# The first loads of a two-layer decoder trunk in another order: identity, one memory tile and one weight slot ahead of the rest

## The chip, the cores and the metric

The kernel runs on one core of one Trainium2 chip. The metric is the device time of one execution in microseconds (us); the time of a kernel is the median of several executions. A profiled execution gives besides its own time the span between its first and last instruction and a record of every instruction and DMA packet.

## The reference, cut to what matters

The program is a decoder trunk of two layers over 256 tokens with 1024 features. The parts that the start of the kernel computes are these:

```python
def memory_attention(q_mem, mem, w_mem_kv):
    kv = mem.astype(q_mem.dtype) @ w_mem_kv
    ...

def gla_group(h, mem, w_in, w_gk_up, b_gk, g_gla, w_mem_kv):
    q, k, v, g_out, gk_low, q_mem = jnp.split(h @ w_in, A_SPLITS, axis=-1)
    gk = jax.nn.log_sigmoid((gk_low @ w_gk_up + b_gk).astype(jnp.float32)) / GLA_GATE_NORM
    o = gla_chunked(q, k, v, gk)          # heads of 96 and 192 features, shapes left out
    o = rmsnorm(o, g_gla) * jax.nn.silu(g_out)
    m = memory_attention(q_mem, mem, w_mem_kv)
    ...

for l in range(2):
    h = rmsnorm(x, g_mix[l])
    mixed = gla_group(...) if l == 0 else diff_group(...)   # the second: differential attention
    x = x + mixed @ w_out[l]
    h = rmsnorm(x, g_ffn[l])
    x = x + (swiglu(h, ...) if l == 0 else moe_swiglu(h, ...))  # the second: top 2 of 8 experts
return rmsnorm(x, g_final)
```

`mem` has 256 rows of 1024 features, `w_mem_kv` is 1024 x 512 per layer, `w_gk_up` is 16 x 384 and `b_gk` has 384 elements.

## The kernel before

**Weights in slots.** Every weight matrix passes through SBUF in slots of 1 MB or less (128 partitions x up to 2048 elements). SP issues the loads into a ring of seven raw buffers (`raw`, semaphores `raw_in`); slot s may be loaded once the lower half of slot s - 7 has been made (`lo_ready`). ScalarE copies a raw slot to `w_hi` in the format fp32r (L395, which drops low bits), VectorE subtracts to get the rest, `w_lo` (L682). There are three such split buffers in the part before the experts, so ScalarE's split of slot s waits until TensorE has used slot s - 3 (`slot_used`). Each product is then three matmuls, hi x hi, lo x hi and hi x lo (`three`, L1130 to L1132).

**Activations.** Activations lie token-major in `H` (two tiles of 128 tokens). A `turn` transposes them on TensorE, eight 128x128 blocks a tile, against the identity `ident`, a block of the constants `cst`; ScalarE copies each half tile to `act_hi` (L406) and VectorE subtracts to `act_lo` (L695), in four quarters: two for each tile. A product that is feature-major waits for three quarters at its first step and for all four at its fifth (`await_turned`).

**The start.** Slots 0 to 3 are `w_mem_kv` of both layers, in halves of 256 columns, slot 4 holds the 16 gate-rank columns of `w_in_a`, slot 5 the memory queries, and slots 6 to 9 the queries and keys of the gated linear attention. The first turn is of `mem`, which SP loads into `H`. While TensorE computes keys and values of the memory from slots 0 to 3, ScalarE and VectorE compute the first layer norm: `norm` on ScalarE squares `xres` (the loaded x) with its sum and takes the root with `eps`, a column of `cst`; `norm` on VectorE waits for the gain (`gain_in`) and writes the result into `H`. On both engines this norm stands between the splits of slots 1 and 2, and each engine works through its program in order. The second turn is that of the normed x.

**Queues.** SP's queue carries all weights, `cst`, `mem` and x. GpSimd's queue carries the gain, broadcast to 128 partitions, and eight small tables that share the semaphore `small_in`: `wgk` (`w_gk_up`), `bgk` (the gate biases as 96 x 4), `ggla`, `gsub` and four lambda vectors, the last six broadcast to 128 partitions. TensorE waits for all eight before the four gate matmuls that follow slots 4 and 5:

```python
pe.wait_ge(small_in, N_SMALL)
for h in range(GH):
    ins = nc.tensor.matmul(ps[0:GDK, 6 + h // 2, S * (h % 2):S * (h % 2) + S],
                           wgk[:, GDK * h:GDK * h + GDK], gd[0:RANK, 0:S], start=True, stop=True)
```

After them ScalarE adds the bias in four operations (L479), and applies Abs, Exp and Ln; VectorE scans. The engines' order within each program is written out by hand.

The rest of the kernel (attention, dense part, shared keys and values, differential attention, router, and eight experts with 42 slots each) is not touched by the diff.

Of the kernel before, what the change touches and what calls it, by code (L numbers as in the profile page):

```python
# [24 lines left out]
P = 128  # L25
D = 1024
S = 256
# [69 lines left out]
def trunk(nc, x, mem, g_mix, g_ffn, w_mem_kv, w_out, w_in_a, w_gk_up, b_gk, g_gla, g_kv, w_kv, w_in_b,  # L97
# [7 lines left out]
    with ExitStack() as ctx:  # L105
# [17 lines left out]
        rsc = sb("rsc", [P, 5, TT, NE])  # L123
        bgk = sb("bgk", [GDK, GH])
        idx8 = sb("idx8", [P, TT, 8], U32)
# [60 lines left out]
        lam4 = sc[:, 0, 0:4 * HEAD_DIM].rearrange("p (i n) -> p i n", i=4)  # L186
        wgk = sc[0:RANK, 1, 0:GH * GDK]

# [14 lines left out]


        const_in = sem("const_in")
        small_in = sem("small_in")
        mem_in = sem("mem_in")
        x_in = sem("x_in")
# [12 lines left out]
        add_done = sem("add_done")  # L221
        gk_logit = sem("gk_logit")
        gk_act = sem("gk_act")
        gk_vec = sem("gk_vec")
# [83 lines left out]
        def _(sp):  # L308
            sp.dma_start(cst[:, :], consts).then_inc(const_in, 16)
            for t in range(TT):  # L310
                sp.dma_start(H[:, t, :], mem[0, P * t:P * t + P, :]).then_inc(mem_in, 16)
            for s, (src, k0, kt, n0, n) in enumerate(slots):
                if s == 2:
                    sp.dma_start(xres[:, :, :], x[0].rearrange("(t p) d -> p t d", p=P)).then_inc(x_in, 16)
                if s >= RAW:
                    sp.wait_ge(lo_ready, s - RAW + 1)
                with nc.allow_non_contiguous_dma(reason="router columns"):
                    sp.dma_start(shaped(raw, s % RAW, kt, n),
                                 src.rearrange("(k p) n -> p k n", p=P)[:, k0:k0 + kt, n0:n0 + n])\
                      .then_inc(raw_in[s % RAW], 16)  # L320
# [36 lines left out]
        def _(pool):  # L357
            gains = [g_mix[0:1, :], g_ffn[0:1, :], g_kv.rearrange("(a d) -> a d", a=1), g_mix[1:2, :],
                     g_ffn[1:2, :], g_final.rearrange("(a d) -> a d", a=1)]
            pool.dma_start(gain[:, :], gains[0].to_broadcast([P, D])).then_inc(gain_in, 16)  # L360
            pool.dma_start(wgk, w_gk_up[0]).then_inc(small_in, 16)
            with nc.allow_non_contiguous_dma(reason="384 gate biases"):
                pool.dma_start(bgk[:, :], b_gk[0].rearrange("(h p) -> p h", p=GDK)).then_inc(small_in, 16)
            pool.dma_start(ggla[:, :], g_gla[0:1, :].to_broadcast([P, GDV])).then_inc(small_in, 16)
# [12 lines left out]
        def _(act):  # L377
# [22 lines left out]

            def turn():
                n = turns[0]
                for t in range(TT):
                    for half in range(2):
# [3 lines left out]
                            ps[:, 2 * t + half, :].rearrange("p (k n) -> p k n", k=4), ACT.Copy).then_inc(turn_hi, 1)  # L408
                turns[0] += 1

# [40 lines left out]
            def attention(u0, u1, slots_end):  # L451
                for i in range(u0, u1 + 4):
# [6 lines left out]
                    if u0 <= i - 4:  # L459
                        unit_square(i - 4)  # L460

            split_to(1)
            turn()
            split_to(2)
            norm(x_in, (16, 16))
            for l in range(2):
# [5 lines left out]
            a = first["in_a"]  # L472

            proj(a + 1, gd[0:RANK, 0:S], ps[0:RANK, 4, 0:S])
            proj(a + 2, qmT[:, :, :], ps[:, 5, :].rearrange("p (m s) -> p m s", m=2))
            act.wait_ge(small_in, N_SMALL)
            act.wait_ge(gk_logit, 1)
            for h in range(GH):
                ins = nc.scalar.activation(ge[:, S * h:S * h + S], ps[0:GDK, 6 + h // 2, S * (h % 2):S * (h % 2) + S],  # L479
                                           ACT.Identity, bias=bgk[:, h:h + 1])  # L480
            ins.then_inc(gk_act, 1)
            act.wait_ge(gk_act, 1)
# [183 lines left out]
        def _(dve):  # L666
# [21 lines left out]

            def turn():
                n = turns[0]  # L690
                for t in range(TT):
                    for half in range(2):
# [4 lines left out]
                            act_hi[:, ks, P * t:P * t + P].bitcast(F32), ALU.subtract).then_inc(turn_lo, 1)  # L697
                turns[0] += 1

# [86 lines left out]
            def head_roots(n):  # L786

                link(nc.vector.reciprocal(hrs[:, n], hrms[:, n]))

            link(nc.vector.memset(ones[:, :], 1.0))  # L790
            link(nc.vector.memset(ki, 1.0))
            link(nc.vector.memset(ki[:, 0:D:CHUNK], 0.0))
            split_to(1)
            turn()
            split_to(2)
# [331 lines left out]
        def _(pe):  # L1127
# [18 lines left out]
            def turn():  # L1146

                for t in range(TT):
                    if turns[0] == 0:
                        pe.wait_ge(mem_in, 16 * TT)  # L1150
                    else:
                        pe.wait_ge(h_ready, TT * (turns[0] - 1) + t + 1)
# [46 lines left out]

            pe.wait_ge(const_in, 16)  # L1200
            turn()
# [16 lines left out]
            for h in range(GH):  # L1218
                ins = nc.tensor.matmul(ps[0:GDK, 6 + h // 2, S * (h % 2):S * (h % 2) + S],
                                       wgk[:, GDK * h:GDK * h + GDK], gd[0:RANK, 0:S], start=True, stop=True)  # L1220
            ins.then_inc(gk_logit, 1)
# [345 lines left out]
```

## Time and profile before

| | |
|---|---|
| median of 3 executions | 1589.26 us (1587.1 to 1592.56) |
| the profiled execution, its own time | 1586.55 us |
| its span | 1584.8 us |
| mean granted TensorE clock over the span | 0.952 |
| bytes moved by DMA | 428.34 MB, mean 270 GB/s |

Times in the trace count from the start of the span. An engine executes its instructions in order, so a row's start is the later of the end of its predecessor and of its waits. PEclk is the share of full TensorE clock that was granted; full is 2.4 GHz and 0.50 is 1.2 GHz. SPq and POOLq are issuing engines: the time beside a DMA issue is that of issuing it, not of the transfer.

### The profile page before, as it was taken

The page shows a single profiled execution, that of the slowest core. Times are in us where ns is not written, and L with a number is a line of the kernel's source. Part 1 is how long each engine was busy: PE and PEld are TensorE (multiplying, and loading weights), DVE is VectorE, ACT ScalarE, POOL GpSimd, SP SyncE. Part 2 cuts the span into 40 slices and gives each one's busy share as a digit, 9 for nine tenths or more (in the row PEclk, how much of TensorE's full clock was granted, in tenths as well). Part 3 has the DMA queues.
Part 4 walks back from the last instruction along what each step waited for, and adds up shares of the span by engine and source line. Part 5 has one row for each costly group of instructions (what it writes and reads, how often), then busy time and mean ns, then how long its engine had stood idle before and what let it go on. Part 6 is the DMA issues. An engine that isn't in the chain of part 4 may idle for free.

```text
span 1584.8 us, 19889 instructions
## 1 busy us (share of the span) xinstructions
PE 1499.1 (95%) x7534; PEld 1252.8 (79%) x7534; DVE 1144.9 (72%) x941; ACT 957.8 (60%) x868; POOL 7.9 (1%) x18
## 2 busy tenths in 40 slices
PE   4997899998978789999999999999999999999996
PEld 4995689998865668888887887887888888888885
DVE  3453454545557479879879878988887987987984
ACT  4553244334445377766767677767767677766773
POOL 1000000000000000000000000000000000000000
PEclk8995799999985899999999999999999999999998
DMA  9561154565512159989989999998997998998990
GB/s 295 184 206 53 54 169 164 187 209 185 165 54 80 53 195 384 387 298 375 387 319 347 385 334 335 384 376 287 394 376 288 384 380 289 385 385 285 380 384 29
DMA packets 201923, 428.34 MB, mean 270 GB/s; under 512 B 8848, under 2 KB 42672, under 8 KB 201872
## 3 DMA queue, kind: packets, MB, share of 16 engines
q1 hardware_dynamic: 200736, 424.18, 74.2%
q0 software_dynamic: 1136, 3.47, 0.9%
q8 instruction: 34, 0.56, 0.1%
q14 instruction: 17, 0.14, 0.0%
HBM read 426.57 MB, written 1.05 MB: 270 GB/s over the span
## 4 chain that ended last, share of the span: by engine, by line
PE 91%; DVE 5%; ACT 2%; DMA 1%; issue 1%; SPq 0%; DVEq 0%; ACTq 0%
PE ps L1130 27%; PE ps L1132 27%; PE ps L1131 27%; PE ps L1448 2%; PE ps L1426 2%; PE ps L1469 2%; DVE w_lo L682 1%; PE ps L1274 1%; DMA raw<-in_w_mem_kv_dram 1%; PE ps L1156 1%; PE ps L1249 1%; ACT w_hi L395 0%; PE ps L1327 0%; DVE small L739 0%; ACT sc L431 0%
## 5 line engine op out<-in xcount | busy, mean ns | idle before, releaser
L1063 DVE TENSOR_TENSOR e_wlo<-raw,e_whi 128x2048 fp32r<-128x2048 f32 x336 | 750.7, 2285 | 113.6 <-ACT e_whi L618 113.4
L618 ACT ACTIVATE e_whi<-raw 128x2048 fp32r<-128x2048 f32 x336 | 620.7, 1915 | 43.5 <-PE ps L1132 43.5
L1130 PE MATMUL ps<-e_whi,act_hi 128*128 128x512 f32 x1344 | 534.4, 398 | 2.9 <-DVE act_lo L1030 1.5
L1132 PE MATMUL ps<-e_wlo,act_hi 128*128 128x512 f32 x1344 | 523.9, 390 | 0.0
L1131 PE MATMUL ps<-e_whi,act_lo 128*128 128x512 f32 x1344 | 523.2, 389 | 0.0
L1130 PEld LDWEIGHTS ps<-e_whi,act_hi 128*128 128x128 f32 x1344 | 252.4, 188 | 57.5 <-issue 5.3
L1131 PEld LDWEIGHTS ps<-e_whi,act_lo 128*128 128x128 f32 x1344 | 252.6, 188 | 54.5 <-issue 3.8
L1132 PEld LDWEIGHTS ps<-e_wlo,act_hi 128*128 128x128 f32 x1344 | 252.3, 188 | 53.5
L682 DVE TENSOR_TENSOR w_lo<-raw,w_hi 128x2048 fp32r<-128x2048 f32 (+2 forms) x68 | 148.4, 2198 | 159.3 <-ACT w_hi L395 159.2
L395 ACT ACTIVATE w_hi<-raw 128x2048 fp32r<-128x2048 f32 (+2 forms) x68 | 124.1, 1839 | 105.7 <-PE ps L1132 89.7
L623 ACT ACTIVATE act_hi<-ps 128x512 fp32r<-128x512 f32 x56 | 33.5, 598 | 199.0 <-PE ps L1469 199.0
L1130 PE MATMUL ps<-act_hi,w_hi 128*128 128x256 f32 (+3 forms) x480 | 137.1, 286 | 14.5 <-DVE act_lo L695 14.5
L1131 PE MATMUL ps<-act_hi,w_lo 128*128 128x256 f32 (+3 forms) x480 | 136.8, 285 | 0.0
L1132 PE MATMUL ps<-act_lo,w_hi 128*128 128x256 f32 (+3 forms) x480 | 136.8, 285 | 0.0
L1130 PEld LDWEIGHTS ps<-act_hi,w_hi 128*128 128x128 f32 (+3 forms) x480 | 89.9, 187 | 16.7 <-issue 16.0
L1131 PEld LDWEIGHTS ps<-act_hi,w_lo 128*128 128x128 f32 (+3 forms) x480 | 90.0, 187 | 0.7
L1132 PEld LDWEIGHTS ps<-act_lo,w_hi 128*128 128x128 f32 (+3 forms) x480 | 89.9, 187 | 0.4
L1130 PE MATMUL ps<-w_hi,act_hi 128*128 128x512 f32 (+1 forms) x240 | 87.5, 365 | 0.2 <-DVE act_lo L695 0.2
L1131 PE MATMUL ps<-w_hi,act_lo 128*128 128x512 f32 (+1 forms) x240 | 87.1, 363 | 0.0
L1132 PE MATMUL ps<-w_lo,act_hi 128*128 128x512 f32 (+1 forms) x240 | 87.0, 362 | 0.0
L544 ACT ACTIVATE T<-ps 128x512 f32<-128x512 f32 x11 | 6.6, 597 | 85.8 <-PE ps L1132 85.8
L1068 DVE TENSOR_TENSOR act_lo<-ps,act_hi 128x512 fp32r<-128x512 f32 x56 | 38.5, 688 | 19.3 <-ACT act_hi L623 19.3
(200 smaller groups left out, 1116.9 us busy)
## 6 DMA issues: line engine op xcount, KB each, us to landing
raw<-in_w_exp_gate_dram SPq DMA_DIRECT2D x112, 1024.0 KB, 7.0
raw<-in_w_exp_up_dram SPq DMA_DIRECT2D x112, 1024.0 KB, 7.2
raw<-in_w_exp_down_dram SPq DMA_DIRECT2D x112, 1024.0 KB, 7.5
raw<-in_w_dense_gate_dram SPq DMA_DIRECT2D x11, 1024.0 KB, 5.2
raw<-in_w_dense_up_dram SPq DMA_DIRECT2D x11, 1024.0 KB, 5.4
raw<-in_w_dense_down_dram SPq DMA_DIRECT2D x11, 1024.0 KB, 5.7
raw<-in_w_out_dram SPq DMA_DIRECT2D x8, 1024.0 KB, 5.0
raw<-in_w_in_a_dram SPq DMA_DIRECT2D x7, 1024.0 KB, 6.6
```

Source lines behind the costliest of these rows:

```text
L395: nc.scalar.activation(w_hi[:, s % SPLIT, 0:kt * n], raw[:, s % RAW, 0:kt * n], ACT.Copy)\
L618: nc.scalar.activation(e_whi[:, (s - NPRE) % E_SPLIT, :], raw[:, s % RAW, :], ACT.Copy)\
L623: nc.scalar.activation(h_hi, ps[:, 4, :].rearrange("p (m n) -> p m n", m=4), ACT.Copy)\
L682: nc.vector.tensor_tensor(w_lo[:, s % SPLIT, 0:kt * n], raw[:, s % RAW, 0:kt * n], w_hi[:, s % SPLIT, 0:kt * n].bitcast(F32), ALU.subtract)\
L1063: nc.vector.tensor_tensor(e_wlo[:, r, :], raw[:, s % RAW, :], e_whi[:, r, :].bitcast(F32), ALU.subtract).then_inc(lo_ready, 1)
L1068: nc.vector.tensor_tensor(h_lo, ps[:, 4, :].rearrange("p (m n) -> p m n", m=4), h_hi.bitcast(F32), ALU.subtract).then_inc(e_lo, 1)
L1130: nc.tensor.matmul(dst, l_hi, r_hi, start=start, stop=False)
L1131: nc.tensor.matmul(dst, l_lo, r_hi, start=False, stop=False)
L1132: return nc.tensor.matmul(dst, l_hi, r_lo, start=False, stop=stop)
L1426: ins = nc.tensor.matmul(ps[:, 1 + 2 * half, P * k:P * k + P], H[:, t, c:c + P], oh[:, t, :], start=(t == 0), stop=(t == TT - 1))
L1448: nc.tensor.matmul(ps[:, SCATTER_BANKS[2 * t + n], :], ohT[:, P * t:P * t + P], y_e[:, 512 * n:512 * n + 512], start=True, stop=True).then ...
L1469: ins = nc.tensor.transpose(ps[:, 4, P * m:P * m + P], e_h[:, P * m:P * m + P], ident)
```

## The change

The constants are loaded in two pieces, the identity first and the remaining 705 columns after slot 1. SP's order becomes identity, memory tile 0, slot 0, memory tile 1, slot 1, other constants, x, slot 2. Each memory tile has a semaphore of its own, so tile 0 can be transposed alone; ScalarE and VectorE take the two quarters of tile 0 ahead of slot 0 and the two of tile 1 behind it. GpSimd issues the gain only when memory tile 1 is in, and the small tables only when x is in. The gate bias is loaded as row 16 under the 16 rows of `wgk`, and a row of ones, set by a memset on VectorE, lies under the gate activations `gd`; so the gate matmuls contract over 17 rows and add the bias, and ScalarE's four bias operations become one copy.

```diff
         lam4 = sc[:, 0, 0:4 * HEAD_DIM].rearrange("p (i n) -> p i n", i=4)
-        wgk = sc[0:RANK, 1, 0:GH * GDK]
+        wgk = sc[0:RANK + 1, 1, 0:GH * GDK]
 
...
 
+        ident_in = sem("ident_in")
         const_in = sem("const_in")
         small_in = sem("small_in")
-        mem_in = sem("mem_in")
+        mem_in = [sem(f"mem_in{t}") for t in range(TT)]
         x_in = sem("x_in")
...
         def _(sp):
-            sp.dma_start(cst[:, :], consts).then_inc(const_in, 16)
-            for t in range(TT):
-                sp.dma_start(H[:, t, :], mem[0, P * t:P * t + P, :]).then_inc(mem_in, 16)
+            with nc.allow_non_contiguous_dma(reason="the identity is a block of the constants"):
+                sp.dma_start(ident, consts[:, C_ID:C_ID + P]).then_inc(ident_in, 16)
+            sp.dma_start(H[:, 0, :], mem[0, 0:P, :]).then_inc(mem_in[0], 16)
             for s, (src, k0, kt, n0, n) in enumerate(slots):
+                if s == 1:
+                    sp.dma_start(H[:, 1, :], mem[0, P:2 * P, :]).then_inc(mem_in[1], 16)
                 if s == 2:
+                    with nc.allow_non_contiguous_dma(reason="the other blocks of the constants"):
+                        sp.dma_start(cst[:, C_IOTA:C_N], consts[:, C_IOTA:C_N]).then_inc(const_in, 16)
                     sp.dma_start(xres[:, :, :], x[0].rearrange("(t p) d -> p t d", p=P)).then_inc(x_in, 16)
...
                      g_ffn[1:2, :], g_final.rearrange("(a d) -> a d", a=1)]
+            pool.wait_ge(mem_in[1], 16)
             pool.dma_start(gain[:, :], gains[0].to_broadcast([P, D])).then_inc(gain_in, 16)
-            pool.dma_start(wgk, w_gk_up[0]).then_inc(small_in, 16)
-            with nc.allow_non_contiguous_dma(reason="384 gate biases"):
-                pool.dma_start(bgk[:, :], b_gk[0].rearrange("(h p) -> p h", p=GDK)).then_inc(small_in, 16)
+            pool.wait_ge(x_in, 16)
+            pool.dma_start(wgk[0:RANK, :], w_gk_up[0]).then_inc(small_in, 16)
+            pool.dma_start(wgk[RANK:RANK + 1, :], b_gk[0:1, :]).then_inc(small_in, 16)
             pool.dma_start(ggla[:, :], g_gla[0:1, :].to_broadcast([P, GDV])).then_inc(small_in, 16)
...
 
-            def turn():
+            def turn(tiles=range(TT)):
                 n = turns[0]
-                for t in range(TT):
+                for t in tiles:
                     for half in range(2):
...
                             ps[:, 2 * t + half, :].rearrange("p (k n) -> p k n", k=4), ACT.Copy).then_inc(turn_hi, 1)
-                turns[0] += 1
+                    turns[0] += t == TT - 1
 
...
 
+            turn(range(0, 1))
             split_to(1)
-            turn()
+            turn(range(1, TT))
             split_to(2)
+            act.wait_ge(const_in, 16)
             norm(x_in, (16, 16))
...
 
+            act.wait_ge(one_row, 1)
             proj(a + 1, gd[0:RANK, 0:S], ps[0:RANK, 4, 0:S])
             proj(a + 2, qmT[:, :, :], ps[:, 5, :].rearrange("p (m s) -> p m s", m=2))
-            act.wait_ge(small_in, N_SMALL)
             act.wait_ge(gk_logit, 1)
-            for h in range(GH):
-                ins = nc.scalar.activation(ge[:, S * h:S * h + S], ps[0:GDK, 6 + h // 2, S * (h % 2):S * (h % 2) + S],
-                                           ACT.Identity, bias=bgk[:, h:h + 1])
-            ins.then_inc(gk_act, 1)
+            nc.scalar.activation(ge.rearrange("p (b n) -> p b n", b=2), ps[0:GDK, 6:8, :], ACT.Copy).then_inc(gk_act, 1)
             act.wait_ge(gk_act, 1)
...
 
-            def turn():
+            def turn(tiles=range(TT)):
                 n = turns[0]
-                for t in range(TT):
+                for t in tiles:
                     for half in range(2):
...
                             act_hi[:, ks, P * t:P * t + P].bitcast(F32), ALU.subtract).then_inc(turn_lo, 1)
-                turns[0] += 1
+                    turns[0] += t == TT - 1
 
...
 
+            nc.vector.memset(gd[0:2 * RANK, 0:S], 1.0).then_inc(one_row, 1)
             link(nc.vector.memset(ones[:, :], 1.0))
...
             link(nc.vector.memset(ki[:, 0:D:CHUNK], 0.0))
+            turn(range(0, 1))
             split_to(1)
-            turn()
+            turn(range(1, TT))
             split_to(2)
...
                     if turns[0] == 0:
-                        pe.wait_ge(mem_in, 16 * TT)
+                        pe.wait_ge(mem_in[t], 16)
                     else:
...
 
-            pe.wait_ge(const_in, 16)
+            pe.wait_ge(ident_in, 16)
             turn()
...
                 ins = nc.tensor.matmul(ps[0:GDK, 6 + h // 2, S * (h % 2):S * (h % 2) + S],
-                                       wgk[:, GDK * h:GDK * h + GDK], gd[0:RANK, 0:S], start=True, stop=True)
+                                       wgk[:, GDK * h:GDK * h + GDK], gd[0:RANK + 1, 0:S], start=True, stop=True)
             ins.then_inc(gk_logit, 1)
```

SP's queue from the start of the program before the change (`H<-in_mem_dram` is the memory, `raw<-in_w_mem_kv_dram` slots 0 to 3, `xres` is x):

```order
L309 DMA cst<-in_consts_dram 128x833
L311 DMA H<-in_mem_dram 128x1024 x2
L318 DMA raw<-in_w_mem_kv_dram 128x8x256 x2
L314 DMA xres<-in_x_dram 128x2x1024
L318 DMA raw<-in_w_mem_kv_dram 128x8x256 x2
L318 DMA raw<-in_w_in_a_dram 128x8x16
```

and with the change:

```order
L311 DMA cst<-in_consts_dram 128x128
L312 DMA H<-in_mem_dram 128x1024
L323 DMA raw<-in_w_mem_kv_dram 128x8x256
L315 DMA H<-in_mem_dram 128x1024
L323 DMA raw<-in_w_mem_kv_dram 128x8x256
L318 DMA cst<-in_consts_dram 128x705
L319 DMA xres<-in_x_dram 128x2x1024
L323 DMA raw<-in_w_mem_kv_dram 128x8x256 x2
L323 DMA raw<-in_w_in_a_dram 128x8x16
```

The identity (128 columns) is alone in front, slot 0 stands between the memory tiles, and the other 705 columns of constants go with x behind slot 1.

ScalarE from the start of its program before the change:

```order
L395 ACT_TABLE_LOAD
L395 ACTIVATE w_hi<-raw 128x2048
L406 ACTIVATE act_hi<-ps 128x4x128 x4
L395 ACTIVATE w_hi<-raw 128x2048
L415 ACTIVATE H,small<-xres 128x1024
L416 ACT_TABLE_LOAD
L416 ACTIVATE small<-small,cst 128x1
L415 ACTIVATE H,small<-xres 128x1024
L416 ACTIVATE small<-small,cst 128x1
```

and with the change:

```order
L412 ACT_TABLE_LOAD
L412 ACTIVATE act_hi<-ps 128x4x128 x2
L401 ACTIVATE w_hi<-raw 128x2048
L412 ACTIVATE act_hi<-ps 128x4x128 x2
L401 ACTIVATE w_hi<-raw 128x2048
L421 ACTIVATE H,small<-xres 128x1024
L422 ACT_TABLE_LOAD
L422 ACTIVATE small<-small,cst 128x1
L421 ACTIVATE H,small<-xres 128x1024
L422 ACTIVATE small<-small,cst 128x1
```

Two of the four act_hi quarters moved ahead of the split of slot 0; the layer norm (rows on `xres` and `small`) stays behind the split of slot 1. VectorE's act_lo quarters move likewise.

## Rows read from the trace of the kernel before

**Rows 1.** The page: engine busy times, and the chain that ended last by engine.

```profile
PE 1499.1 (95%) x7534; PEld 1252.8 (79%) x7534; DVE 1144.9 (72%) x941; ACT 957.8 (60%) x868; POOL 7.9 (1%) x18
...
PE 91%; DVE 5%; ACT 2%; DMA 1%; issue 1%; SPq 0%; DVEq 0%; ACTq 0%
```

**Rows 2.** Chain that ended last, 0 to 30 us: start, duration, what.

```profile
2.14 15.84 DMA raw<-in_w_mem_kv_dram
...
18.00 1.92 ACT w_hi L395
...
20.02 2.29 DVE w_lo L682
22.31 1.81 DVE act_lo L695 x3
...
24.25 0.55 PE ps L1130
```

**Rows 3.** Timeline of TensorE, 9 to 13 us: start, duration, what, idle before.

```profile
9.30 3.65 PE L1156 MATMUL ps<-cst,H 128*128 128x128 f32 x16 [9.30 <-DMA H<-in_mem_dram]
```

**Rows 4.** Timeline of SP's queue, 0 to 200 us.

```profile
0.75 0.40 SPq L309 DMA_DIRECT2D cst<-in_consts_dram  x1
1.20 0.90 SPq L311 DMA_DIRECT2D H<-in_mem_dram  x2
2.14 2.42 SPq L318 DMA_DIRECT2D raw<-in_w_mem_kv_dram  x2
4.60 8.30 SPq L314 DMA_DIRECT2D xres<-in_x_dram  x1
```

**Rows 5.** DMA queues from 8.5 to 13.5 us: packets, MB, share of 16 engines.

```profile
DMA packets 441, 0.46 MB, mean 93 GB/s; under 512 B 61, under 2 KB 382, under 8 KB 441
...
q0 software_dynamic: 120, 0.13, 75.6%
q1 hardware_dynamic: 321, 0.33, 19.2%
```

**Rows 6.** DMA from 14 to 18 us.

```profile
DMA packets 1402, 1.45 MB, mean 363 GB/s; under 512 B 37, under 2 KB 1379, under 8 KB 1402
```

**Rows 7.** DMA issues, 0 to 14 us: KB each, us to landing (median).

```profile
xres<-in_x_dram SPq DMA_DIRECT2D x1, 1024.0 KB, 18.8
gain<-in_g_mix_dram POOLq DMA_DIRECT2D x1, 512.0 KB, 7.4
cst<-in_consts_dram SPq DMA_DIRECT2D x1, 416.5 KB, 3.1
...
sc<-in_lambda_k_dram POOLq DMA_DIRECT2D x2, 32.0 KB, 9.2
```

**Rows 8.** Timeline of ScalarE, 27.5 to 70 us.

```profile
33.06 1.91 ACT L395 ACTIVATE w_hi<-raw 128x2048 fp32r<-128x2048 f32 x1 [3.59 <-PE ps L1132]
...
44.57 1.92 ACT L395 ACTIVATE w_hi<-raw 128x2048 fp32r<-128x2048 f32 x1 [4.96 <-PE ps L1132]
...
64.05 1.55 ACT L479 ACTIVATE T<-ps,bgk 96x256 f32<-96x256 f32 x4
65.64 1.06 ACT L483 ACTIVATE T<-T 96x1024 f32<-96x1024 f32 x1
```

**Rows 9.** Windows: length, busy by engine; PEclk, DMA share, GB/s.

```profile
24.00:30.50 6.50, 6.25 (x29) 6.28 (x30) 6.43 (x8) 5.41 (x8) 0.51 (x1) 0.51 1.05 311
30.50:41.00 10.50, 10.50 (x90) 10.50 (x89) 3.98 (x3) 3.19 (x4) 0.03 (x1) 1.00 1.09 342
60.00:70.00 10.00, 10.00 (x78) 9.16 (x77) 2.25 (x3) 7.76 (x10) 0.00 (x0) 1.00 0.71 228
```

**Rows 10.** Timeline of VectorE, 27.5 to 32 us.

```profile
29.61 2.28 DVE L682 TENSOR_TENSOR w_lo<-raw,w_hi 128x2048 fp32r<-128x2048 f32 x1
```

**Rows 11.** Timeline of GpSimd's queue, 0 to 30 us.

```profile
1.91 0.51 POOL L361 DMA_DIRECT2D sc<-in_w_gk_up_dram  x1
...
5.78 0.54 POOL L367 DMA_DIRECT2D sc<-in_lambda_k_dram  x1
```

More of the change, by code:

```diff
@@ L123, in trunk @@
         rsc = sb("rsc", [P, 5, TT, NE])
-        bgk = sb("bgk", [GDK, GH])
         idx8 = sb("idx8", [P, TT, 8], U32)
@@ L222, in trunk @@
         gk_logit = sem("gk_logit")
+        one_row = sem("one_row")
         gk_act = sem("gk_act")
```

## The prediction

> **What bounds the kernel now.** I read the page first: TensorE is busy 95% of the span and holds 91% of the chain that ended last [rows 1]. So time can only go where TensorE waits. The longest such wait is the first one, and all moved instructions lie there, so I read the chain of waits from zero next: the first weight slot is issued at 2.14 us and lands at 18.00; ScalarE's upper half of it takes 1.92, VectorE's lower half 2.29, three of the four act_lo quarters 1.81, and the first product starts at 24.25 [rows 2]. The two memory tiles were there long before: the transposes start at 9.30, when the second tile lands [rows 3]. So the slot's landing releases everything, and the question is why 1 MB takes 15.8 us.
>
> The issues on SP's queue say what is ahead of it: the constants (416.5 KB), both tiles (1 MB), then slots 0 and 1, then x, whose issue is held until 12.9 [rows 4]. The queues say what happens beside it. Between 8.5 and 13.5 us q0, which carries GpSimd's tables, holds 75.6% of the sixteen engines' time for 120 packets and 0.13 MB; q1, with the weights, gets 19.2% and moves 0.33 MB [rows 5]. From 14 to 18, with q0 nearly empty, the mean is 363 GB/s [rows 6]. At that rate q1 would have moved 1.8 MB in those 5 us, so the table loads cost about 1.5 MB, or 4.1 us, just ahead of slot 0's landing. The four 32 KB lambda broadcasts are the last, landing 9.2 us after issue [rows 7].
>
> After 24.25 TensorE is continuously fed: ScalarE's splits at 33.06 and 44.57 start only when TensorE has used up a slot [rows 8], and the stretch 60 to 70 is full [rows 9]. A TensorE that starts earlier therefore keeps its lead, if slots keep coming.
>
> **The change part by part.** *Slot 0 lands earlier.* Ahead of its end stand 64 + 512 + 1024 KB, 1.64 MB, and no GpSimd transfer, since the gain waits for tile 1. The old constants, 0.43 MB, were in at 0.75 + 3.1 = 3.85 [rows 4, 7]. I let the new order have moved the same 0.43 MB by then; the other 1.21 MB at 363 GB/s take 3.3: 7.2 us, and I take 7.4 because the slowest engine ends a transfer. Upper bound: 1.48 MB were in only at 9.30 before, with q0 alongside [rows 3]; with the missing 0.16 MB that is 9.75. No row excludes 7.2 as the lower one.
>
> *The chain behind it.* ScalarE's two and VectorE's two quarters of tile 0 now lie before slot 0: tile 0 is in near 4.3, eight transposes are half of 3.65 [rows 3], done by 6.2, its copies by 6.9. After the landing: 1.92 + 0.10 + 2.29, then only one quarter instead of three, 0.60, and 0.13 of hand-over: 5.04 instead of 6.25. Tile 1 lands near 7.2 + 1.4 = 8.7, its first quarter is copied by 10.3, while VectorE is still in w_lo until 11.7. First product: 7.4 + 5.04 = 12.4. Against 24.25 that is 11.8 us earlier; with the bounds, 9.5 to 12.0.
>
> *Does the lead survive slot 2?* Before it stands the layer norm. x now follows 4.63 MB of its own queue and shares with 0.52 MB of gain: 3.85 + 4.72/0.363 = 16.9. The gain, issued near 8.8, took 7.4 before [rows 7], so 16.2: no later than x. Before, x landed at 4.60 + 18.8 = 23.4 and slot 2's lower half ended at 29.61 + 2.28 = 31.9, 8.5 later [rows 4, 7, 10]; so now 25.4. TensorE wants slot 2 where it wanted it before, 11.8 earlier: two slots took 44.57 - 33.06 = 11.5 [rows 8], so slot 2 began at about 38.6, now 26.8. Slack 1.4: no stall, but little more lead would be usable. The second constants transfer (352 KB) is within these bytes and the sqrt that reads its eps comes after x.
>
> *And slot 3?* It lands near 22.7 (two more MB at 363). Its limit: TensorE wants it at 44.3 - 11.8 = 32.5, less 4.4 for both halves: 28.1. The deferred tables start when x is in. Before, 6.6 us passed from the first table issue at 1.91 [rows 11] to the slow stretch; so it comes at 23.5 to 28.5. If slot 3 is caught by all of its 4.1 us it lands at 26.8, still 1.3 in time. Its cover is the 5.75 us that each slot feeds TensorE.
>
> *The rest.* The tables are first read by the gate matmuls, ahead of ScalarE's bias step at 64.05 [rows 8], now near 52. Their eight issues take 5.78 - 1.91 [rows 11], so the last comes near 21, and with 9.2 it lands at 30. Hidden by 20 us; until x is in, GpSimd holds nothing else back, its next gain being wanted only after the first layer norm's reader. The bias row replaces four ScalarE operations, 1.55 together, by one of 96x1024, like the Abs at 1.06 [rows 8]: 0.5 less on ScalarE, while TensorE is full with the next slots [rows 9]; without that cover it would be a gain of 0.5, so the bounds are 0 and 0.5 and I take 0. The matmuls' 17 rows instead of 16: no row shows it; the moving columns are the same, I take 0. The 32x256 memset stands ahead of VectorE's first wait, under the loads: 0. The extra issue on SP: 0.45 us, as between the first two [rows 4], already behind slot 0.
>
> *The clock.* 24.0 to 30.5 was granted 0.51, the lower level, 1.2 GHz: 29 matmuls in 6.25 us, 0.216 each; afterwards, at 1.00, 90 in 10.5, 0.117 each [rows 9]. How long the low level lasts behind the new start no row tells. Bounds: not at all, 29 x 0.099 = 2.9 less, and twice as long, 2.9 more; I take the same.
>
> Sum: 1586.55 - 11.8 = 1574.8 for the profiled execution. That one lies 2.7 below the median of the three runs, 1589.26, so the median becomes 1577.5.
>
> **A rule weighed.** What the trace shows is that SP's slot lands late while q0's packets occupy the engines [rows 5]. The Trainium skill, DMA: Bandwidth & Descriptors, section Queues, rings and completion order, says that each engine takes turns between queue rows packet by packet, and that a transfer's semaphore write lands after all earlier writes of that engine, across queues; by that rule the trace agrees, and it speaks against the change as much as for it, since deferred tables hold up slots 2 and 3 in the same way: that is rival A. The same page, Rules for kernel authors, advises coalescing small transfers, under 64 KB being mostly overhead, and the 64 KB identity is cut out of a larger one: rival B.
>
> **The rivals.** *A, the slow stretch stalls slot 3.* For: it must fall somewhere. Against: 1.3 us of slack after its full price. Were it twice as long (8.2), slot 3 would land at 30.9, 2.8 late: 1580.3.
> *B, the split costs in series.* SP's landings overlap (issues 0.45 apart), against it. Were the identity's fixed time paid ahead of tile 0, slot 0 would be later by at most 3.1 - 1.2 = 1.9, cst's time from issue to landing [rows 7] less 1.2 for its bytes: 1579.4. Bytes and slot 0 shift alike, so nothing gives this back.
> *C, the slow stretch belongs to slot 0's own first reads,* not to the tables. For: its packets begin in that stretch. Against: q0's 75.6%. Then slot 0 takes from tile 0's landing (4.3) the 8.7 it took from 9.30 to 18.00: 13.0, gain 5.0 + 1.2: 1583.1.
> *D, the clock is high from the first product:* 2.9 less, but slot 2 would then be wanted at 23.9 and comes at 25.4, which gives 1.5 back: 1576.1.
> *E, slower: the clock stays low.* TensorE now begins with two separate bursts of eight transposes and may be granted 1.2 GHz through slots 0 to 3. From 30.4 to 50 some 168 matmuls x 0.099 = 16.6 more: 1594.1. It decides from 119 matmuls on. Against: before, the level rose after 6.1 us of products from the same idle start.
>
> **How the numbers follow.** My forecast, 1577.5, has 73% (its own range 1574 to 1580.5); A 8%, B 5%, C 6%, D 5%, E 3%. The range takes in A to D, the bound of 9.75 for slot 0 (1579.8) and 2 us for the spread of a median (the three runs span 5.5): 1572 to 1583. Faster means over 0.3%, 4.8 us, about what a measurement of this kernel can tell from no change: below 1584.5. The main case and A to D lie there, except late ends of C: 92% faster, 5% the same, 3% slower.
>
> **What would show it.** Right: slot 0's split on ScalarE near 7.4, the first product near 12.4, slot 3's chain without a wait on a DMA, ScalarE's gate step near 52 and every later stage 11 to 12 earlier. A: a ScalarE wait on raw behind slot 2 and a TensorE gap near 32. C: 1 KB loads slow with q0 empty. E: PEclk near 0.5 beyond 20. Wrong as a whole: later stages that do not move with the first.

## The result and the profile after

The changed kernel takes 1597.8 us (median of 4 executions, 1596.49 to 1598.68) against 1588.18 (1585.01 to 1592.56): ratio 1.0058, 95% interval 1.0032 to 1.0084. It is 0.6% slower, where a gain to 1577.5 was forecast. The profiled execution took 1597.82 with a span of 1596.0, so its span is 11.2 longer than that of before.

The start went nearly as forecast. The chain that ended last, over the first microseconds, answers to [rows 2]:

```profile
1.66 6.89 DMA raw<-in_w_mem_kv_dram
8.58 1.92 ACT w_hi L401
10.52 2.29 DVE w_lo L687
12.82 0.61 DVE act_lo L700
...
13.56 0.55 PE ps L1137
14.11 0.21 PE ps L1138
...
17.32 0.21 PE ps L1138
17.53 0.19 PE ps L1139
...
21.34 0.12 PE ps L1138
```

Slot 0 lands at 8.55 instead of 17.98, 6.89 us behind its issue instead of 15.84; one act_lo quarter stands between its lower half and the first product instead of three, and that product starts at 13.56 instead of 24.25. The matmuls step by 0.21 us until 17.5 and by 0.12 afterwards; the granted column reads 1.00 from 13.5 on in this trace, so here the steps tell the level, not the column: before, 0.216 us a matmul stood beside a granted 0.51, and 0.117 beside 1.00 [rows 9]. The tables' slow stretch is now at 22 to 27, in the DMA queues of that window:

```profile
DMA packets 1631, 0.81 MB, mean 163 GB/s; under 512 B 1040, under 2 KB 1575, under 8 KB 1631
...
q0 software_dynamic: 191, 0.24, 60.8%
q1 hardware_dynamic: 1440, 0.57, 43.2%
```

q0 holds 60.8% of the engines' time for 0.24 MB (the next gain is in it too), much as it did at 8.5 to 13.5 before [rows 5]. Not all of this stretch is the tables': 1040 packets in it are under 512 B, where it was 61 before, since slot 4, 16 columns wide, is read here in packets of 64 B. ScalarE's timeline, which answers to [rows 8]:

```profile
23.85 1.92 ACT L401 ACTIVATE w_hi<-raw 128x2048 fp32r<-128x2048 f32 x1 [0.18 <-DMA raw<-in_w_mem_kv_dram]
...
34.04 1.92 ACT L401 ACTIVATE w_hi<-raw 128x2048 fp32r<-128x2048 f32 x1 [6.23 <-DMA raw<-in_w_in_a_dram]
...
51.93 1.01 ACT L486 ACTIVATE T<-ps 96x1024 f32<-96x1024 f32 x1
52.97 1.06 ACT L488 ACTIVATE T<-T 96x1024 f32<-96x1024 f32 x1
```

Slot 3's split waited 0.18 us for its load, slot 5's 6.23, and neither made TensorE late: its one wait between 14 and 52 us is 1.44 us behind the second turn, and the kernel before has the same one. The gate step starts at 51.93 instead of 64.05: by then the kernel is 12.1 us ahead. The lead is still there when the experts start. The first and the last gather of the experts, `ps<-oh,H`, are given by the view of tile oh, with the change:

```profile
L1433 PE MATMUL ps<-oh,H x256: 275/275/579, 553.7 to 1449.7; 128*128 128x128 f32 x128
```

and of before:

```profile
L1426 PE MATMUL ps<-oh,H x256: 274/275/582, 565.3 to 1441.4; 128*128 128x128 f32 x128
```

First gather 553.7 against 565.3, 11.6 us ahead; last gather 1449.7 against 1441.4, 8.3 behind. The 896.0 us between them took 876.1 before: 19.9 us are lost there, with TensorE busy throughout and the clock granted in full. From the first gather to the end of the span it is 11.6 + 11.2 = 22.8 us, since the last expert's products follow the last gather. Two windows between those gathers, before and then after (columns as in [rows 9]):

```profile
565.00:1441.00 876.00, 874.15 (x4022) 719.45 (x4023) 750.57 (x469) 627.16 (x443) 0.00 (x0) 1.00 0.96 353
```

```profile
554.00:1450.00 896.00, 894.50 (x4027) 719.87 (x4027) 750.64 (x465) 629.93 (x442) 0.00 (x0) 1.00 0.94 345
```

And the groups by line say in what. The three matmuls of each expert product, mean ns of one, before:

```profile
L1130 PE MATMUL ps<-e_whi,act_hi 128*128 128x512 f32 x1344 | 534.4, 398 | 2.9 <-DVE act_lo L1030 1.5 <-DVE act_lo L1068 1.4
L1132 PE MATMUL ps<-e_wlo,act_hi 128*128 128x512 f32 x1344 | 523.9, 390 | 0.0
L1131 PE MATMUL ps<-e_whi,act_lo 128*128 128x512 f32 x1344 | 523.2, 389 | 0.0
```

and after:

```profile
L1137 PE MATMUL ps<-e_whi,act_hi 128*128 128x512 f32 x1344 | 541.9, 403 | 2.9 <-DVE act_lo L1037 1.5 <-DVE act_lo L1075 1.4
L1139 PE MATMUL ps<-e_wlo,act_hi 128*128 128x512 f32 x1344 | 531.4, 395 | 0.0
L1138 PE MATMUL ps<-e_whi,act_lo 128*128 128x512 f32 x1344 | 531.4, 395 | 0.0
```

Each of the 1344 triples costs 5 + 5 + 6 ns more, 21.5 us together, although the instructions, their shapes, their data and the clock are the same. (`ps<-e_whi,act_hi` names the tile that is streamed first and the tile of the stationary blocks second.) Their weight loads (PEld) take 188 ns in both. So the question was what an edit of the first 60 us, or of the gate bias, does to a matmul a thousand microseconds later.

### The profile page after: what moved, and what is told of

It is laid out like the page before. It is cut to its first block, busy times and chain, and to the rows that moved or that the text cites. A ratio compares the mean times of both kernels' runs of the same rounds, so it can differ in the third digit from the quotient of the medians.

```text
span 1596.0 us, 19888 instructions
## 1 busy us (share of the span) xinstructions
PE 1521.3 (95%) x7534; PEld 1248.0 (78%) x7534; DVE 1145.8 (72%) x942; ACT 961.3 (60%) x865; POOL 7.7 (0%) x18
## 4 chain that ended last, share of the span: by engine, by line
PE 92%; DVE 5%; ACT 2%; issue 1%; DMA 0%; SPq 0%; DVEq 0%; ACTq 0%
PE ps L1137 27%; PE ps L1139 27%; PE ps L1138 27%; PE ps L1455 2%; PE ps L1433 2%; PE ps L1476 2%; DVE w_lo L687 1%; PE ps L1281 1%; PE ps L1163 1%; PE ps L1256 1%; DVE H L715 0%; ACT w_hi L401 0%; PE ps L1334 0%; DVE small L744 0%; DMA raw<-in_w_mem_kv_dram 0%
## 5 line engine op out<-in xcount | busy, mean ns | idle before, releaser
L1137 PE MATMUL ps<-e_whi,act_hi 128*128 128x512 f32 x1344 | 541.9, 403 | 2.9 <-DVE act_lo L1037 1.5
L1139 PE MATMUL ps<-e_wlo,act_hi 128*128 128x512 f32 x1344 | 531.4, 395 | 0.0
L1138 PE MATMUL ps<-e_whi,act_lo 128*128 128x512 f32 x1344 | 531.4, 395 | 0.0
L1139 PEld LDWEIGHTS ps<-e_wlo,act_hi 128*128 128x128 f32 x1344 | 252.5, 188 | 60.8
```

Source lines behind the costliest of these rows:

```text
L1137: nc.tensor.matmul(dst, l_hi, r_hi, start=start, stop=False)
L1138: nc.tensor.matmul(dst, l_lo, r_hi, start=False, stop=False)
L1139: return nc.tensor.matmul(dst, l_hi, r_lo, start=False, stop=stop)
```

## The experiments

One line of the diff, its first, is not in the cut shown above: the tile `bgk`, 96 x 4 elements, is no longer declared. Tiles are laid out in the order of their declarations, so everything declared behind it moves down. The addresses in the built programs, in bytes of a partition:

```
tile               before    changed
act_hi              75776      75776
act_lo              83968      83968
bgk (16 of 32)     117376          -
w_hi and e_whi     118784     118752
w_lo               143360     143328
e_wlo              167936     167904
```

The 16 bytes of `bgk` take up 32, so all that lies behind it moves down by 32. Theory A: the place of the weight tiles costs the 20 us. Rivals: the expert part runs slower because it starts at another phase (B), or because of the bias row or the new semaphores (C).

**Room for bgk.** The changed kernel with one more unused tile:

```diff
+        sb("bgk_room", [P, 4])
         idx8 = sb("idx8", [P, TT, 8], U32)
```

> The changed kernel with 32 bytes of unused room where the 16-byte tile bgk stood, so that every tile behind it, w_hi, w_lo, e_whi and e_wlo among them, lies at its old address; order of loads and work as in the changed kernel. Theory A (addresses): the loss is in the matmuls that stream a weight tile of 512 columns, since all weight tiles moved down by 32 bytes; then the expert matmuls on e_whi go back from 403, 395 and 395 ns to 398, 390 and 389, the 12.1 us won by the 50th microsecond stay, and the time is 1588.2 - 12 = 1576 us. Rival B (phase): the expert part runs slower because it starts 12 us earlier against the ring of loads or the clock; then room changes nothing: 1597 to 1598 us, 403 ns. Rival C (the row of biases or the third semaphore costs later): also 1597 to 1598.

Measured: 1577.33 us, ratio 0.9932 (0.9909 to 0.9955). The expert matmuls of this kernel:

```profile
L1138 PE MATMUL ps<-e_whi,act_hi 128*128 128x512 f32 x1344 | 534.5, 398 | 2.9 <-DVE act_lo L1038 1.5 <-DVE act_lo L1076 1.4
L1140 PE MATMUL ps<-e_wlo,act_hi 128*128 128x512 f32 x1344 | 524.0, 390 | 0.0
L1139 PE MATMUL ps<-e_whi,act_lo 128*128 128x512 f32 x1344 | 523.2, 389 | 0.0
```

Between the gathers 558.9 to 1435.9, 877.0 us. Theory A held to the nanosecond. B and C fell: this kernel starts as early as the changed one and has its row of biases and its semaphores.

**The shift alone.** The kernel before, with nothing else touched:

```diff
-        sb("split_pad", [P, 280])
+        sb("split_pad", [P, 272])
```

> The kernel before with the unused tile split_pad 32 bytes shorter, so that w_hi, w_lo, e_whi and e_wlo lie 32 bytes lower as in the changed kernel; no load and no instruction moved. Theory A: the expert matmuls go from 398, 390, 389 ns to 403, 395, 395, and the time to 1588.2 + 23 = 1611 us, while the first product stays at 24.25 us. Rivals B and C: 1588 us, unchanged.

Measured: 1607.68 us, ratio 1.0134 (1.0109 to 1.0158), expert matmuls 403, 395 and 395 ns:

```profile
L1130 PE MATMUL ps<-e_whi,act_hi 128*128 128x512 f32 x1344 | 541.9, 403 | 2.9 <-DVE act_lo L1030 1.5 <-DVE act_lo L1068 1.4
L1132 PE MATMUL ps<-e_wlo,act_hi 128*128 128x512 f32 x1344 | 531.4, 395 | 0.0
L1131 PE MATMUL ps<-e_whi,act_lo 128*128 128x512 f32 x1344 | 531.3, 395 | 0.0
```

Gathers from 562.5 to 1458.3, 895.8 us. The 32 bytes are enough for the whole loss: about 20.5 us over the kernel before here, and 20.5 between the changed kernel and the one with room. I had expected 1611, 23 us more. The profiled execution has the whole 22.7 in its expert part, but reaches the first gather 2.8 us early, and that comes from its first 61 us: slot 0 landed at 16.9 and the clock rose at 26, so the gate step is at 61.06 instead of 64.05. From the gate step to the first gather it takes 501.4 us, as before (501.3).

**Tables deferred, order kept.**

```diff
+            pool.wait_ge(x_in, 16)
             pool.dma_start(wgk, w_gk_up[0]).then_inc(small_in, 16)
```

> The kernel before, all addresses kept, with one edit: GpSimd waits for x before it issues the eight small tables; the order on SP's queue is that of before. If the tables' slow packets delay slot 0, it lands after 3.04 MB (2.52 of SP and 0.52 of gain): near 11 us instead of 18.0, the first product is at 17.3 instead of 24.25 and the time is 1581 us. If the slow stretch belongs to slot 0's own reads (rival C of the prediction), slot 0 stays near 18 and the time at 1588.

Measured: 1583.13 us, ratio 0.9971 (0.9958 to 0.9985). From 8.5 to 13.5 us the queues now read:

```profile
DMA packets 1788, 1.81 MB, mean 363 GB/s; under 512 B 20, under 2 KB 1787, under 8 KB 1788
...
q1 hardware_dynamic: 1787, 1.81, 109.1%
q0 software_dynamic: 1, 0.00, 0.0%
```

363 GB/s in that stretch against 93 before [rows 5], with slot 0's 1 KB reads in it: the slow stretch belongs to the tables, and rival C of the prediction is refuted. Slot 0 is split at 12.21, the first product at 18.47, 5.8 us earlier, a microsecond short of what was expected.

**Order changed, tables not deferred.** The changed kernel with room for bgk and without GpSimd's two waits:

```diff
-            pool.wait_ge(mem_in[1], 16)
             pool.dma_start(gain[:, :], gains[0].to_broadcast([P, D])).then_inc(gain_in, 16)
-            pool.wait_ge(x_in, 16)
             pool.dma_start(wgk[0:RANK, :], w_gk_up[0]).then_inc(small_in, 16)
```

> The changed kernel with the old addresses (room as in the first run) and without GpSimd's two waits: gain and tables are issued at the start again. Slot 0 then shares with the gain and lands near 9 to 10 us, just ahead of the slow stretch of 8.5 to 13.5: first product near 14.5, 9 to 10 earlier. The slow stretch falls on slot 1 and x: x lands near 21, the layer norm behind it makes slot 2 ready near 29.5 where TensorE wants it near 29, so the time is about 1579 us. If deferral matters as much as the order, 1583 or more.

Measured: 1584.93 us, ratio 0.9983 (0.9970 to 0.9996); slot 0's split only at 16.45, the first product at 21.43. I was wrong by 7 us there: the slow stretch caught the end of slot 0, again from 8.5 to 13.5 us,

```profile
q0 software_dynamic: 121, 0.13, 61.9%
q1 hardware_dynamic: 319, 0.40, 32.1%
```

and q1 moved 0.40 MB in 5 us. Of the lead of 10.7 at the first product the order alone brings 2.8 and the deferral alone 5.8; the rest needs both. In the times it is 2.3 and 4.1 us alone, and 9.9 together (the version with room). The Trainium skill, DMA: Bandwidth & Descriptors, section Queues, rings and completion order, has each engine take turns between queues packet by packet; by that rule a 1 MB slot that is nearly done still waits at each turn for a slow packet of the other queue, and the trace agrees: q0 held 61.9% of the engines' time for 121 packets, and slot 0 came only when they were through.

**Is it the place or the distance?** A matmul of an expert product streams a weight tile, and in the trace the loads of stationary blocks from act_hi or act_lo (PEld) overlap the matmuls. So two tiles are read at once, and three runs move one, the other, or both. Each was executed once. The edits to the changed kernel (both at -32; activations alone at -32; weights at -64):

```diff
-        sb("act_pad", [P, 480])        # both, and activations alone
+        sb("act_pad", [P, 472])
...
-        sb("split_pad", [P, 280])
+        sb("split_pad", [P, 288])      # both; 296 for activations alone; 272 with act_pad kept for -64
```

> The changed kernel with act_pad 32 bytes shorter and split_pad 32 bytes longer: act_hi, act_lo and all up to the constants lie 32 bytes lower than in the kernel before, and the weight tiles stay 32 bytes lower too, so the distance between stationary and streamed tiles is the old one. If the 6 ns of an expert matmul come from the distance between the two tiles read at once, they go: 398, 390, 389 ns and about 1577 us. If they come from the place of the streamed weight tile itself, they stay: 403, 395, 395 ns and 1597 us.

> The changed kernel with the weight tiles back at their old address and act_hi, act_lo and all up to the constants 32 bytes lower. Distance theory: 403, 395, 395 ns in the expert matmuls, 1597 us. Place-of-the-streamed-tile theory: the expert matmuls, which stream weights, keep 398, 390, 389 and 1577 us, while the 256-column matmuls that stream act_hi may move by 2 or 3 ns (480 x 3 of them, 3 to 4 us).

> The changed kernel with the weight tiles 64 bytes lower than in the kernel before instead of 32. If any place off the old one costs the same, 403, 395, 395 ns and 1597 us. If the cost grows with the distance from it, about 409 ns and 1620 us; if 32 bytes is special (64-byte places are good), 398, 390, 389 and 1577 us.

Both tiles 32 bytes lower: 1577.89 us, and

```profile
L1137 PE MATMUL ps<-e_whi,act_hi 128*128 128x512 f32 x1344 | 534.6, 398 | 2.9 <-DVE act_lo L1037 1.5 <-DVE act_lo L1075 1.4
L1139 PE MATMUL ps<-e_wlo,act_hi 128*128 128x512 f32 x1344 | 524.0, 390 | 0.0
L1138 PE MATMUL ps<-e_whi,act_lo 128*128 128x512 f32 x1344 | 523.2, 389 | 0.0
```

The activations alone, weight tiles at their old place: 1599.43 us, and

```profile
L1137 PE MATMUL ps<-e_whi,act_hi 128*128 128x512 f32 x1344 | 541.5, 403 | 2.9 <-DVE act_lo L1037 1.5 <-DVE act_lo L1075 1.4
L1139 PE MATMUL ps<-e_wlo,act_hi 128*128 128x512 f32 x1344 | 530.7, 395 | 0.0
L1138 PE MATMUL ps<-e_whi,act_lo 128*128 128x512 f32 x1344 | 530.6, 395 | 0.0
```

So the place of the streamed tile means nothing by itself; the distance between the two does. Each time rests on one execution, but the loss is over 20 us and the means are of 1344 matmuls each. With the weights at -64 it was 1592.91 us, with 403, 395 and 395 ns again: the same step, not twice. (Its time is lower than the changed kernel's because it reached its first gather at 548.0; see below.)

**A larger distance.** The changed kernel with `split_pad` at 32 elements, which puts all weight tiles 1024 bytes below their place in the kernel before.

> The changed kernel with all weight tiles 1024 bytes below their old place, so the distance from act_hi to e_whi is an odd multiple of 1024 bytes. If any multiple of 1024 (or of 64 and more, short of 32 and 64 themselves) does, 398, 390, 389 ns in the expert matmuls and 1577 us; if only whole multiples of 2048 bytes do, 403, 395, 395 and 1593 to 1598 us.

Measured: one execution, 1581.11 us, expert matmuls 398, 390 and 389 ns. A whole 1024 does no harm. In the kernel before the distances from act_hi and act_lo to e_whi and e_wlo are all whole multiples of 2048 bytes (43008, 34816, 92160 and 83968); 32 or 64 off cost the 5 to 6 ns (64 with the weights lower, 32 also with the activations lower), and 1024 off nothing.

No run puts the expert tiles between 64 and 1024 off, but every trace holds one such distance. The dense part's last product streams w_hi in 512 columns against f_hi, and f_hi at 218368 lies 99584 bytes above w_hi: 256 over a whole 1024. Both move together, so it is the same before and after:

```profile
L1130 PE MATMUL ps<-w_hi,f_hi 128*128 128x512 f32 x88 | 34.4, 391 | 0.3 <-DVE w_lo L682 0.3
L1137 PE MATMUL ps<-w_hi,f_hi 128*128 128x512 f32 x88 | 34.4, 391 | 0.3 <-DVE w_lo L687 0.3
```

391 ns, and 227 from one start to the next (median), which is the step of the expert matmuls at their good distance too; 32 off they step at 233. So 256 over costs nothing here.

**The part before the experts wants the opposite for 256 columns.** Many of its products stream act_hi in 256 columns, with the stationary blocks in w_hi and w_lo. Their groups, before and then after:

```profile
L1130 PE MATMUL ps<-act_hi,w_hi 128*128 128x256 f32 (+3 forms) x480 | 137.1, 286 | 14.5 <-DVE act_lo L695 14.5
L1131 PE MATMUL ps<-act_hi,w_lo 128*128 128x256 f32 (+3 forms) x480 | 136.8, 285 | 0.0
```

```profile
L1137 PE MATMUL ps<-act_hi,w_hi 128*128 128x256 f32 (+3 forms) x480 | 135.1, 281 | 5.3 <-DVE act_lo L700 5.3
L1138 PE MATMUL ps<-act_hi,w_lo 128*128 128x256 f32 (+3 forms) x480 | 134.7, 281 | 0.0
```

285 to 286 ns became 280 to 281, and the median step 117 instead of 120. It is the number of columns that turns the sign, not the exchanged roles. With w_hi streamed and act_hi stationary, as in the expert products, 256 columns get shorter and 512 longer; before:

```profile
L1130 PE MATMUL ps<-w_hi,act_hi 128*128 128x256 f32 x64 | 18.1, 283 | 0.0
L1130 PE MATMUL ps<-w_hi,act_hi 128*128 128x512 f32 x176 | 69.4, 395 | 0.2 <-DVE act_lo L695 0.2
```

and after:

```profile
L1137 PE MATMUL ps<-w_hi,act_hi 128*128 128x256 f32 x64 | 18.0, 281 | 0.0
L1137 PE MATMUL ps<-w_hi,act_hi 128*128 128x512 f32 x176 | 70.8, 402 | 0.2 <-DVE act_lo L700 0.2
```

The steps are 120 and 117 ns with 256 columns, 227 and 235 with 512. So the shift wins little in this part: some 1600 matmuls of 256 columns x 3 ns are nearly 5 us, and 528 of 512 columns x 6 to 8 take 3 to 4 of them back, which leaves about 1. So a version was made with old places for the expert tiles alone:

```diff
+        sb("e_pad", [P, 8])
         e_whi = sb("e_whi", [P, E_SPLIT, SLOT], F32R)
```

> The changed kernel with 32 bytes of room ahead of e_whi alone: the expert tiles e_whi and e_wlo at their old places, w_hi and w_lo of the part before the experts 32 bytes lower, as in the changed kernel. Address theory: expert matmuls at 398, 390, 389 ns, the expert part (first to last gather) 877 us as with all old addresses instead of 896, and the 256-column matmuls before it keep their shorter step, 117 instead of 120 ns. The first gather then starts near 554 us as in the changed kernel instead of 559, and the time is 1573 us, 4 below the version with all old addresses. Rival: the 5 us between those two starts are the clock's windows and not the addresses; then 1577 us.

Measured: 1575.62 us, ratio 0.9921 (0.9907 to 0.9934); first gather at 554.8, last at 1430.4. The interval reaches from 1573 to 1577, so the time does not choose between the theory and the rival. And with w_hi and w_lo at -64 (`split_pad` 272, `e_pad` 16):

> The changed kernel with w_hi and w_lo of the part before the experts 64 bytes below their old places and the expert tiles e_whi and e_wlo at their old ones. In the run with all weight tiles 64 bytes lower the first gather of the experts came at 548.0 us against 554.8 with 32, and the expert part from its first to its last gather took 896.7 us; with the expert tiles at a distance of whole 2048 bytes from act_hi it took 876 to 877. If both hold together: first gather at 548, last at 1424, time 1570 us. If the 6.8 us of the start were the clock's windows in that one run, 1575 us like the version with 32.

Measured: 1575.24 us, ratio 0.9909 (0.9892 to 0.9926), first gather at 554.4, not 548: the early start of that single run with -64 did not return. Both versions beat the kernel before and the changed one; from the version with all old addresses (0.9909 to 0.9955) they can't be told apart by time. Their first gather comes 4 us earlier than in that version's profiled execution, but that one, at 1581.23 us, was the slowest of its four; two other runs at whole distances (both tiles lower, old bias) reach it at 557.3 and 556.9, 2 to 3 us behind. By the steps about 1 us of that is due to the addresses; the rest is not shown to be.

**The turns split.** The changed kernel with room for bgk and, on ScalarE and VectorE:

```diff
-            turn(range(0, 1))
             split_to(1)
-            turn(range(1, TT))
+            turn()
```

> The changed kernel with all old addresses and the turn of both memory tiles behind slot 0's split again, as before. The prediction's term: two act_lo quarters more between slot 0's lower half and the first product, 1.2 us: first product 6.2 us behind slot 0's landing instead of 5.0, near 14.7 instead of 13.5, and 1.2 us more in all. Rival (the split of the turns buys nothing since tile 1 arrives late anyway): 13.5.

Measured: one execution, 1582.74 us, and in its chain that ended last three quarters again:

```profile
8.53 1.92 ACT w_hi L402
10.55 2.29 DVE w_lo L687
12.84 1.81 DVE act_lo L700 x3
...
14.78 0.55 PE ps L1136
```

6.25 us from ScalarE's start to the product instead of 4.98: the term is 1.27. The time itself, 5.4 above the version with room, is that of one execution and is not read.

**The bias in its old form.** The changed kernel with `bgk`, its load, its four operations and the matmuls over 16 rows:

```diff
-            pool.dma_start(wgk[RANK:RANK + 1, :], b_gk[0:1, :]).then_inc(small_in, 16)
+                pool.dma_start(bgk[:, :], b_gk[0].rearrange("(h p) -> p h", p=GDK)).then_inc(small_in, 16)
...
-            nc.scalar.activation(ge.rearrange("p (b n) -> p b n", b=2), ps[0:GDK, 6:8, :], ACT.Copy).then_inc(gk_act, 1)
+            for h in range(GH):
+                ins = nc.scalar.activation(ge[:, S * h:S * h + S], ps[0:GDK, 6 + h // 2, S * (h % 2):S * (h % 2) + S],
+                                           ACT.Identity, bias=bgk[:, h:h + 1])
```

> The changed kernel with the bias in its old form: the 96 x 4 tile bgk, its load, and four ScalarE operations of 1.55 us instead of one of 1.01; bgk stands at its old place, which puts all addresses back. Prediction's step: the 0.5 us lie under full TensorE work, so the first product stays at 13.5 and the time is that of the version with all old addresses, 1577 us (single runs of it: 1575.5 to 1581.2). If the bias row were what slows the expert part: 1577 too, but with the new form at old addresses then slow, which it was not; so only a gain or loss at the gate itself is left, and a loss of 0.5 would show as TensorE idle behind the four gate matmuls.

Measured: one execution, 1577.55 us; the four operations take 1.55 us from 52.08, the gate matmuls 1.96 from 50.02, and TensorE goes on at 51.91 without idle time. So the form of the bias makes no difference that this run shows; it was the room of `bgk` that mattered.

## Why the prediction was wrong

**The step that failed** is the one by which the rest of the kernel only moves: "A TensorE that starts earlier therefore keeps its lead", and in the change part by part there is no term at all for the removed declaration. The bias row was costed as "0.5 less on ScalarE", with bounds 0 and 0.5. Its true price was the vacated room: 19.9 us between the expert gathers, 22.8 to the end of the span, shown by putting the room back (1577.33) and by moving the weight tiles alone in the kernel before (1607.68). No rival named it, the range ended at 1583, and 92% stood on faster.

**The mechanism that was forecast was right, but its gain was smaller.** With the old addresses the time is 1577.33, where the forecast was 1577.5. That agreement is partly luck. The forecast took 11.8 us off a kernel before of 1589.26, the median of three; beside the version with room the kernel before measured 1587.23, so the gain is 9.9. The terms of the start, measured on the changed kernel: slot 0 in at 8.55 instead of 7.4, first product at 13.56 instead of 12.4, the chain between them 4.98 for 5.04, x in at 17.7 for 16.9, slot 2's lower half done at 26.0 for 25.4, slot 3 in at 23.85 for 22.7, the tables' slow stretch at 22 to 27 for 23.5 to 28.5, the gate step at 51.93 for 52.

The last is luck too. Slot 0 came 1.1 us late, and two things that the sum did not have made that good in this execution. The matmuls stepped at 0.21 us only from 13.56 to about 17.6, not for the 6.1 us of before: 19 matmuls (4.1 us at 0.216) instead of 29, ten at 0.099 less, 1.0 us. And the some 250 matmuls of 256 columns that follow up to the gate step took 3 ns less each because of the very shift of addresses. In the version with room the low level lasted until 18.9, the steps were 120 ns, and the gate step came at 52.89.

**Rivals.** A: the stretch delayed slots 3 and 5 at ScalarE only; no stall. B: slot 0 needed 6.89 us, so the identity's fixed time is at most in the 1.1. C: refuted by the tables' deferral alone. D and E: neither; the steps fell to 0.12 us after 4 us and stayed there through slots 0 to 3. The rival on the slower side was a clock that stays low, and the result fell there for another reason.

**The lead in the middle.** That it is kept was only partly right even at old addresses. The windows of the version with room, from 109 to 559 us, and of before, 120 to 565 (the ends are the same places of the program within a microsecond):

```profile
109.00:559.00 450.00, 401.96 (x2247) 340.86 (x2247) 230.62 (x362) 182.41 (x295) 2.11 (x4) 0.84 0.37 122
```

```profile
120.00:565.00 445.00, 395.27 (x2247) 335.79 (x2246) 229.94 (x358) 181.92 (x295) 2.13 (x4) 0.86 0.37 123
```

450 us for the work of 445, at a granted 0.84 instead of 0.86: of 11.2 us at the gate step (52.89 against 64.05) 6.4 are left at the first gather. In the run with only the tables deferred it was 6.2 and 1.6. Both traces are of the slowest execution of their kernel, so they show more of this loss than a median one has; but in the runs with both tiles lower and with the old bias, at 1577.89 and 1577.55 us, some 3.6 us are lost too. From the gate step to the first gather the seven runs at whole distances with a changed start take 504.5 to 506.1 us, where the kernel before takes 501.3. These are the stretches in which TensorE works in small pieces and the clock goes up and down; where it does so moved with the start. That this and nothing else takes the 3 to 5 us was not tried apart. The runs with w_hi 32 or 64 bytes off take 501.4 to 502.8 (the single one with all weights at -64: 497.7), of which the matmul steps explain under 1 us.

## What to carry to other kernels

A removed or added tile moves every tile behind it, and that alone cost 20 us here. Where a kernel has unused tiles with odd sizes its addresses may be part of its tuning: compare the addresses before pricing any edit of the declarations, and put the room back when one goes. When a matmul group's mean changes by some ns with shape, clock and count the same, ask for the distance between the streamed and the stationary tile. In a list of loads, what stands on another queue counts too: ahead of the first weights neither the order nor the deferral of the slow broadcasts brought the gain alone.

## What the runs showed of the hardware that had not been expected

Matmuls of 512 streamed columns took 398, 390 and 389 ns in the expert products where the distance between the tile streamed and the tile of stationary blocks was a whole multiple of 1024 bytes (the kernel before and nine of the experiments), and 403, 395 and 395 where it was 32 or 64 bytes off (the changed kernel, the shift alone, activations alone, -64). Against f_hi, 256 bytes over a whole 1024, 512 columns took 391, so not every other distance costs. Matmuls of 256 columns did the reverse, whichever tile was streamed: 285 to 288 ns with act_hi streamed at whole distances, 280 to 284 off them, and with w_hi streamed 283 at whole ones, 279 to 281 at 32 off and 276 to 277 at 64. Which part of the memory or the engine is behind it no run tells.

Eight broadcast and small table loads of 0.32 MB took up much of the sixteen engines for some 5 us in each of three places (q0's share 75.6% at 8.5 to 13.5 us before, 61.9% with the order changed alone, 60.8% at 22 to 27 after, there with part of the next gain).
